# Where the activation operand of the matmuls starts in SBUF: a start 12 bytes lower, off the 32-byte grid

## The reference

```python
u = h @ a_w_in[i]
x = x + mix @ w_out[l]
return jnp.square(jax.nn.relu(h @ w_in)) @ w_out
u = causal_depthwise_conv(h @ w_up[i], conv_w[i], conv_b[i])
```

## Time and profile before

| | us |
|---|---|
| median of 3 runs | 1023.32 |
| the runs | 1022.25, 1024.44, 1023.32 |
| the profiled execution, its own time | 1023.86 |
| its span, first to last instruction | 1022.1 |
| TensorE (PE) busy in the span | 987.7 (97%) |
| VectorE (DVE) busy | 759.3 (74%) |
| ScalarE (ACT) busy | 609.7 (60%) |
| GpSimd (POOL) busy | 160.1 (16%) |
| mean granted TensorE clock | 0.989 of full speed |

### The profile page before, as it was taken

How to read it: one execution, slowest core, us unless ns; L and a number is a source line. 1 busy time by engine, 2 the same in 40 slices (tenths; PEclk the granted TensorE clock), 3 DMA queues, 4 the chain that set the end, 5 groups by cost and what they waited for, 6 DMA issues and landing times.

```text
span 1022.1 us, 18048 instructions
## 1 busy us (share of the span) xinstructions
PE 987.7 (97%) x6987; PEld 884.7 (87%) x6987; DVE 759.3 (74%) x1429; ACT 609.7 (60%) x1143; POOL 160.1 (16%) x87
## 2 busy tenths in 40 slices
PE   8999999999999998899989999999999999999996
PEld 5989888888899985598878889998788999999876
DVE  4798779877867767766987676677576788867786
ACT  6645557564646767756647464566555656545465
POOL 2953102122200000000221220102000000201201
PEclk9999999999999999999999999999999999999998
DMA  9582154654545440044555555422405345554511
GB/s 370 192 245 84 46 202 165 213 200 170 201 168 204 170 167 1 1 143 167 186 196 181 200 180 192 173 89 80 165 1 196 122 179 197 175 206 158 183 73 42
DMA packets 25428, 160.50 MB, mean 157 GB/s; under 512 B 2944, under 2 KB 5248, under 8 KB 7296
## 3 DMA queue, kind: packets, MB, share of 16 engines
q1 hardware_dynamic: 24912, 158.28, 43.4%
q10 hardware_dynamic: 432, 1.07, 0.3%
HBM read 157.86 MB, written 1.49 MB: 156 GB/s over the span
## 4 chain that ended last, share of the span: by engine, by line
PE 83%; DVE 11%; ACT 3%; issue 2%; DMA 1%; POOLq 0%; DVEq 0%; ACTq 0%
PE bank L760 79%; PE obank L760 3%; DVE split_lo L622 2%; PE bank L923 1%; DVE tmp L2250 1%; DVE tmp L2242 1%; ACT probs L1581 1%; DMA x<-in_x 1%; DVE hidden_parts L2242 1%; DVE rowmax L2794 0%; DVE square_sum L2242 0%; DVE act_parts L2250 0%; DVE probs L2246 0%; DVE x L2242 0%; ACT act_parts L1584 0%
## 5 line engine op out<-in xcount | busy, mean ns | idle before, releaser
L614 ACT ACTIVATE split_hi<-ring 128x1024 fp32r<-128x1024 f32 (+1 forms) x280 | 290.1, 1049 | 116.7 <-PE bank L760 116.7
L760 PE MATMUL bank<-act_parts,split_hi 128*128 128x256 f32 (+1 forms) x1696 | 316.3, 288 | 5.0 <-DVE act_parts L2242 2.3
L622 DVE TENSOR_TENSOR split_lo<-ring,split_hi 128x1024 fp32r<-128x1024 f32 (+1 forms) x221 | 269.8, 1230 | 29.2 <-ACT split_hi L614 28.6
L760 PEld LDWEIGHTS bank<-act_parts,split_hi 128*128 128x128 f32 x1696 | 263.3, 190 | 13.0 <-issue 5.9
L760 PE MATMUL bank<-hidden_parts,split_hi 128*128 128x512 f32 (+1 forms) x944 | 263.1, 346 | 2.9 <-DVE split_lo L622 2.6
L622 POOL TENSOR_TENSOR split_lo<-ring,split_hi 128x1024 fp32r<-128x1024 f32 (+1 forms) x59 | 143.5, 2440 | 721.1 <-ACT split_hi L614 719.9
L760 PE MATMUL bank<-act_parts,split_lo 128*128 128x256 f32 x880 | 247.5, 281 | 0.0
L760 PE MATMUL bank<-hidden_parts,split_lo 128*128 128x256 f32 x752 | 211.4, 281 | 0.0
L760 PEld LDWEIGHTS bank<-hidden_parts,split_hi 128*128 128x128 f32 x944 | 163.7, 188 | 26.1 <-DVE split_lo L622 3.2
L760 PE MATMUL bank<-mlp_parts,split_hi 128*128 128x512 f32 x512 | 178.7, 391 | 1.1 <-DVE mlp_parts L2250 1.1
L760 PEld LDWEIGHTS bank<-act_parts,split_lo 128*128 128x128 f32 x880 | 168.4, 191 | 0.0
(11 more groups left out here) (272 smaller groups left out, 1179.1 us busy)
## 6 DMA issues: line engine op xcount, KB each, us to landing
ring<-in_weights SPq DMA_DIRECT2D x140, 1024.0 KB, 4.8
ring<-in_weights SPq DMA_DIRECT2D x5, 768.0 KB, 4.2
ring<-in_weights SPq DMA_DIRECT2D x3, 512.0 KB, 4.7
shifted<-conv_rows SPq DMA_DIRECT2D x9, 142.0 KB, 5.1
x<-in_x ACTq DMA_DIRECT2D x2, 512.0 KB, 7.7
y<-in_mem SPq DMA_DIRECT2D x1, 1024.0 KB, 12.0
out<-x SPq DMA_DIRECT2D x4, 256.0 KB, 2.9
consts<-in_consts SPq DMA_DIRECT2D x1, 933.0 KB, 13.5
```

The source lines that it names most:

```text
L614: nc.scalar.activation(split_hi[:, w % SPLIT, 0:n], src, ACT.Copy).then_inc(sem("high_parts"), 1)
L622: (nc.vector if engine == "vector" else nc.gpsimd).tensor_tensor(split_lo[:, w % SPLIT, 0:n], src, split_hi[:, w % SPLIT, 0:n].bitcast(F32 ...
L760: return nc.tensor.matmul(dst, lhsT, rhs, start=start, stop=stop)
```

## The change

The tensors `apart` and `act_parts` become one, `act_room`, and `act_parts` is the view of it that begins 45 words in.

```diff
-        apart = sb("apart", [128, 48])
-        act_parts = sb("act_parts", [128, 2, KD, SEQ], F32R)
+        act_room = sb("act_room", [128, 2 * KD * SEQ + 45], F32R)
+        act_parts = act_room[:, 45:].rearrange("p (a k t) -> p a k t", a=2, k=KD)
         behind_act = sb("behind_act", [128, 24])
```

## The result

| | before | after |
|---|---|---|
| runs together, median us | 1023.88 (1022.25 to 1029.49, 4 runs) | 1036.77 (1033.12 to 1038.50, 4 runs) |
| the profiled execution, us | 1023.86 | 1035.39 |
| its span, us | 1022.1 | 1033.6 |

The ratio is 1.0111, with a 95% interval of 1.0062 to 1.0161: slower by 6 to 16 us. The forecast was 1017.3 us, faster by 6.

What follows compares the result with a forecast made beforehand. TensorE was taken as the bound, busy 97% of the span and 83% of the chain. Elementwise 0, matmul rate 6.1 us less and DMA 0 summed to -6 us: 1017.9 from 1023.86, median 1017.3; range 1012.5 to 1030.0.

Steps and rivals of the forecast that it cites:

- Term 1: Elementwise instructions that read or write `act_parts`, 480 ns on VectorE and 497 on ScalarE: taken as 0, bounded by 4 us.
- Where the effect would be and how to read it: Only in the speed of single instructions touching `act_parts`; matmul rate to be read as distance from start to start.
- DMA and waits: DMA and the rest of the kernel: nothing moves, no wait is added, 0 us.
- Term 2: Rate of the `act_parts` matmuls: 1356 of them go from 117.8 to 113.3 ns, 6.1 us less.
- fast pace: The quicker of two rates of 256-column matmuls on `act_parts` in the trace: 113.3 ns from start to start.
- four long streams: `act_parts` matmul stretches at 117.8 ns: 192 from 440.2 us, 768 from 790, 288 from 905.3, 108 from 997.
- slow meeting: Weight load and moving operand reads starting on the same grid in each `act_parts` matmul, at 117.8 ns; a shift would spoil it.
- The step before it: `act_parts` matmuls with the same operands run at 113.3 or 117.8 ns, and a pace, once taken, is held.
- rival of the extra fetch: A moving operand starting inside a four-word piece needs one more fetch: 1.8 ns a matmul, 4.7 us, 1028.0 us; chance 0.18.
- rival of the slow pace everywhere: Some 800 `act_parts` matmuls at 113.3 ns fall back to 117.8: 3.6 us, 1026.9, or 1031.6 us with extra fetch; chance 0.16.
- The independent ports: By the skill's rule, weight loads take nothing from the running matmul: matmul rate change 0, 1023.3 us; the trace disagreed.

Runs made afterwards that it cites:

- the measurement alone: Whole computation left out; TensorE alone issues the kernel's matmuls at 64 starts of the activations, weights at 96, later 100 to 112; threes took 113.3 to 123.9 ns.
- 28 words: `act_parts` begins 28 words into the room, at 208 modulo 256, all else as in the kernel before: 1022.91 us against 1023.40, ratio 0.9988.

## Why the prediction was wrong

**Term 1, the elementwise instructions at 0: right.** They stayed at 479 and 499 ns.

**Where the effect would be and how to read it: right.** Of all steady distances between matmul starts only those on `act_parts` changed, and they account for 11.0 of 11.5 us; the other tensors' matmuls kept their pace to 0.1 ns. DMA and waits, at 0, were right in the net: what is left is 0.5 us.

**Term 2, the pace after the change: wrong, in sign.** I took the fast pace of 113.3 ns on the four long streams, because the shift would take the moving stream off the grid on which both start and so spoil the slow meeting. Being off the grid is itself the cost: 120.8 ns, above both paces that the trace had. In the measurement alone a start at 4 modulo 16 gives 121.5 ns in the mean where one at 0 gives 117.9, and 121.2 to 121.8 against 117.8 to 118.7 for the other four starts of the weights. The step that failed is the argument that a regular stream is helped by an irregular start; no row of the profile bore it, and the text said so and put it first all the same.

**The step before it, that a pace is the stream's own: half wrong.** A pace is held once taken, but which one is taken changes from one execution of the same program to the next: the stream from 795 us ran at 117.8 ns in one and at 113.4 in two. Even had the mechanism been right, 3.5 of the 6.1 us (768 x 4.5 ns) hung on what one execution out of three showed. The prediction had seen two paces at one address and still built its sum on the paces of a single profile.

**The rival of the extra fetch: right in kind, too small.** It asked for 1.8 ns a matmul and 1028.0 us. The three kinds of start inside 16 bytes should then cost alike; 4 bytes in cost 3.6 ns, 8 bytes 2.1, 12 bytes 0.2 (weights at 96). One more line for each stream is thus not the mechanism, or not alone. The Trainium skill (SBUF — State Buffer, in Door 1: The DMA port swizzle) gives SBUF lines of 16 bytes, with a penalty for each access that crosses to a new one. The runs agree as far as the period of the grid goes: 0 modulo 16 and 0 modulo 32 are alike (113.7 and 114.6 at the same distance), 4 modulo 16 is not. Why a start at 12 modulo 16 costs nothing it does not say.

**The rival of the slow pace everywhere** gave 1026.9, or 1031.6 with the extra fetch; the profiled execution's 1035.4 lies above both. Its size of 4.5 ns applied to some 800 fast matmuls; in fact all 2360 rose.

**The independent ports.** The Trainium skill (TensorE: Matmul & The Clock Gate, Part 2: What happens when you issue a matmul) has the weight load and the moving operand on two independent ports, so that a load takes nothing from the running matmul. By that rule the weights' start should not matter to the stream. It does: `mlp_parts` did not move, and its pairs went from 115.6 ns in every run with the weights at 96 to 117.7 when the weights alone moved by 12 bytes (`splits3`). Whether the two meet at the ports or elsewhere no run tells.

**The range** ended at 1030.0, and the upper bound of the pace was the slow one plus 1.8 ns, 119.6, for an operand at a kind of start of which no row existed. It should have been left open further.

What stays open is by what mechanism a start at 4 or 8 modulo 16 costs time while one at 12 does not, why the distance matters as it does on the grid, and what makes a stream settle at 113.3 or 117.8 ns from the same starts. No run here tells.

## What to carry to other kernels

Let an fp32r operand that TensorE streams start on a multiple of 16 bytes, and look at it when a view is cut out of a larger buffer, since the values are the same either way. That avoids the cost of a start at 4 or 8; it does not make the stream fast by itself (113.3 to 123.3 ns on the grid). Read a matmul stream's pace from start to start, in more than one profiled execution, before a plan is built on it: the same program took two. Hold stages of two executions against each other only where their granted clocks are alike. Where a placement is to be tuned, a sweep of the stream alone found in two runs what eight single placements had only hinted at, and it carried over to the kernel. What a better pace is worth has to be worked out against several executions of the kernel as it is.

## What the runs showed of the hardware that was not expected

- An fp32r matmul of 256 columns with a weight load each runs at 113.3 to 123.9 ns from start to start at 320 pairs of starts of its two operands in SBUF, each measured once, no other engine being busy.
- A start of the moving operand 4, 8 and 12 bytes past a multiple of 16 costs 3.6, 2.1 and 0.2 ns (threes) and 3.2, 2.3 and -0.6 ns (pairs), in the mean over 16 starts each with the weights at 96 modulo 256.
- For the weights such a start costs nothing of its own on the mean: 117.8 to 118.7 ns for weights 0, 4, 8, 12 and 16 bytes further, with the moving operand on a line.
- For some placements the pace has several steady values, and one execution may hold another than the next (113.3 or 117.8 ns before, 120.0 or 123.3 in the change); others settled at one value in every long stream (113.3 in both profiles with 28 words).
